# Turning x as it lands, the norm's root taken at the copy out of the in-projection, and the first conditioning chunks moved behind it

## The reference

```python
def rmsnorm(x, g):
    return x * rsqrt(mean(x * x, axis=-1) + RMS_EPS) * g

h = rmsnorm(x, g_attn_norm)                  # 256 x 1024
proj = h @ w_in                              # 1024 x 928
u, q_lat, kv_lat, k_r = split(proj, (512, 256, 128, 32))
q  = rmsnorm(q_lat,  g_q_a)  @ w_q_b         # the next product
kv = rmsnorm(kv_lat, g_kv_a) @ w_kv_b
```

## Time and profile before

| | us |
|---|---|
| median of 3 runs (lowest, highest) | 1545.74 (1544.13, 1547.88) |
| the profiled execution, device time | 1543.98 |
| its span, first to last instruction | 1542.1 |
| TensorE busy | 1459.0 (95% of the span) |
| VectorE, ScalarE, GpSimd busy | 324.6, 221.6, 21.5 |
| mean granted clock of TensorE | 0.976 |

### The profile page before, as it was taken

How to read it: one execution, slowest core, us unless ns; L and a number is a source line. 1 busy time by engine, 2 the same in 40 slices (tenths; PEclk the granted TensorE clock), 3 DMA queues, 4 the chain that set the end, 5 groups by cost and what they waited for, 6 DMA issues and landing times.

```text
span 1542.1 us, 18050 instructions
## 1 busy us (share of the span) xinstructions
PE 1459.0 (95%) x7280; PEld 791.3 (51%) x7280; DVE 324.6 (21%) x862; ACT 221.6 (14%) x405; POOL 21.5 (1%) x14
## 2 busy tenths in 40 slices
PE   7998999999999999999999999999699998999998
PEld 5654443343443343343343343343599664888843
DVE  5526321121111111121121121111323534000001
ACT  1321011011111111111011011011223420100000
POOL 3100000000000000000000000000000000000000
PEclk9998999999999999999999999999899868999999
DMA  9996999999999999999999999999844002444300
GB/s 330 357 416 272 380 427 430 428 428 429 428 428 429 428 428 429 428 428 428 428 429 429 428 428 428 428 428 408 259 156 145 28 27 83 158 143 143 131 0 27
DMA packets 82570, 496.96 MB, mean 322 GB/s; under 512 B 6237, under 2 KB 47914, under 8 KB 54666
## 3 DMA queue, kind: packets, MB, share of 16 engines
q1 hardware_dynamic: 81932, 495.46, 79.0%
q10 hardware_dynamic: 606, 1.06, 0.2%
HBM read 495.44 MB, written 1.05 MB: 322 GB/s over the span
## 4 chain that ended last, share of the span: by engine, by line
PE 61%; DMA 34%; DVE 3%; issue 1%; ACT 1%; SPq 0%; DVEq 0%; ACTq 0%
DMA ring<-in_w_gate_up_dram 33%; PE PS L816 16%; PE PS L1004 10%; PE PS L554 8%; PE PS L842 5%; PE PS L1020 5%; PE PS L802 3%; PE PS L708 3%; PE PS L850 2%; PE PS L657 2%; PE PS L537 1%; PE PS L683 1%; PE PS L510 1%; DMA ring<-in_w_ada_dram 1%; ACT work L1170 0%
## 5 line engine op out<-in xcount | busy, mean ns | idle before, releaser
L816 PE MATMUL PS<-ring,work 128*64 128x512 f32 x2048 | 450.7, 595 | 13.9 <-DMA ring<-in_w_gate_up_dram 13.9
L816 PEld LDWEIGHTS PS<-ring,work 128*64 128x64 f32 x2048 | 142.7, 137 | 304.2 <-issue 260.9
L842 PE MATMUL PS<-ring,work 128*64 128x512 f32 x1024 | 225.1, 592 | 0.0
L1643 DVE TENSOR_SCALAR work<-PS 128x512 f32<-128x512 f32 x32 | 22.1, 691 | 659.9 <-PE PS L816 659.9
L1004 PE MATMUL PS<-ring,cols 128*128 128x256 f32 x704 | 156.7, 384 | 2.1 <-issue 2.1
L1004 PEld LDWEIGHTS PS<-ring,cols 128*128 128x128 f32 x704 | 135.1, 193 | 21.0 <-DVE cols L1349 2.5
L842 PEld LDWEIGHTS PS<-ring,work 128*64 128x64 f32 x1024 | 71.6, 137 | 132.1 <-issue 129.6
L802 PE MATMUL PS<-work,rows 128*128 128x64 f32 x1056 | 124.9, 278 | 1.0 <-DVE work L1621 1.0
L802 PEld LDWEIGHTS PS<-work,rows 128*128 128x128 f32 x1056 | 123.8, 196 | 1.9 <-DVE work L1621 1.9
L554 PE MATMUL PS<-ring,cols 128*128 128x240 f32 (+3 forms) x576 | 117.1, 364 | 4.1 <-DVE cols L1349 2.1
L554 PEld LDWEIGHTS PS<-ring,cols 128*128 128x128 f32 x576 | 107.0, 190 | 12.1 <-DVE cols L1349 2.5
(11 more groups left out here) (264 smaller groups left out, 860.1 us busy)
## 6 DMA issues: line engine op xcount, KB each, us to landing
ring<-in_w_gate_up_dram SPq DMA_DIRECT2D x128, 2048.0 KB, 22.4
ring<-in_w_down_dram SPq DMA_DIRECT2D x64, 2048.0 KB, 19.5
ring<-in_w_ada_dram SPq DMA_DIRECT2D x24, 1024.0 KB, 16.9
ring<-in_w_gate_up_dram SPq DMA_DIRECT2D x22, 1024.0 KB, 5.1
ring<-in_w_in_dram SPq DMA_DIRECT2D x13, 960.0 KB, 10.8
ring<-in_w_down_dram SPq DMA_DIRECT2D x11, 1024.0 KB, 4.8
ring<-in_w_out_dram SPq DMA_DIRECT2D x8, 1024.0 KB, 10.0
ring<-in_w_in_dram SPq DMA_DIRECT2D x3, 1024.0 KB, 12.8
```

Source lines behind the costliest of these rows:

```text
L816: mm = pe.matmul(bank(b)[CAP * h:CAP * (h + 1), :], xg[:, k, :], w[:, b * FE + h * 512:b * FE + (h + 1) * 512], start=False, stop=(k == KD ...
L842: mm = pe.matmul(bank(3)[CAP * h:CAP * (h + 1), :], lhs, w[:, (f % 2) * D + h * 512:(f % 2) * D + (h + 1) * 512], start=False, stop=(f == 7))
L1643: v.tensor_scalar(g_min, bank(0), LIMIT, None, ALU.min).then_inc(clipped, 1)
```

## The change

1. x is turned on TensorE as it was loaded, half by half, without the norm (`turn_x`), and `cols` is x's transpose with the gain alone.
2. The sum of squares of the first half is taken by VectorE, that of the second by ScalarE. One inverse root of two columns is computed behind `keep_cols` and announced as `attn_r`. ScalarE applies it when it copies the in-projection's chunks out, in two instructions for a chunk (one for each half of the tokens) where it was one.
3. `cst`'s first part is loaded ahead of x.
4. `ADA_FIRST` is 0: the four w_in chunks take ring places 0 to 3, and conditioning chunks 0 to 3 take 4 to 7. TensorE computes all four between the latents' transposes and the product with w_q_b. The places from 8 on stay as they were.
5. Counts of semaphores are adapted, and `bias14_in` is merged into `gfin_in`.

```diff
-ADA_FIRST, ADA_NEXT, ADA_MID = 2, 4, 18
+ADA_FIRST, ADA_NEXT, ADA_MID = 0, 4, 18
...
+            load_small(cst[:, 0:CONST_FIRST], consts[:, 0:CONST_FIRST], "const_in")
             load_small(x_sb[:, 0, :], x_rows[:, 0, :], "x0_in")
             load_small(x_sb[:, 1, :], x_rows[:, 1, :], "x1_in")
-            load_small(cst[:, 0:CONST_FIRST], consts[:, 0:CONST_FIRST], "const_in")
...
+            def turn_x():
+
+                for t in range(NT):
+                    pe.wait_ge(sig[("x0_in", "x1_in")[t]], 16)
+                    for k in range(KD):
+                        mm = pe.transpose(bank(k // 2)[:, (k % 2) * T + t * P:][:, 0:P],
+                                          x_sb[:, t, k * P:(k + 1) * P], ident)
+                        if t == NT - 1 and k % 2:
+                            mm.then_inc(sig["rows_turned"], 1)
+                turned[0] += 1
...
             pe.wait_ge(sig["const_in"], 16)
+            turn_x()
             pe.wait_ge(sig["vec_in"], 2 * 16)
...
-            for i in range(ADA_FIRST):
-                ada(i)
...
-            turn_rows(2)
             need_cols()
             project(IN1_CHUNKS, N_IN1, (4, 5), 0)
...
+            act.wait_ge(sig["x1_in"], 16)
+            do.tell(nc.scalar.activation(rows[:, 1, :], x_sb[:, 1, :], ACT.Square,
+                                         accum_out=stat(ms, S_ATTN)[:, 1:2]), "x_squared")
             act.wait_ge(sig["vec_cols"], 1)
+            keep_cols(lambda k: col("g_attn_norm", k))
             a = VEC_ROWS["c_2"][0]
             do.tell(nc.scalar.activation(c_rep[:, :, :], vcol[:, a:a + KD].unsqueeze(2).to_broadcast([P, KD, 32]),
                                          ACT.Silu), "c_ready")
-            keep_cols(lambda k: col("g_attn_norm", k))
...
-            keep_proj(proj1, IN1_CHUNKS, (4, 5), N_IN1)
+            act.wait_ge(sig["attn_r"], 1)
+            for c, (a, w) in enumerate(IN1_CHUNKS):
+                act.wait_ge(chunk_used, N_IN1 + c + 1)
+                for t in range(NT):
+                    ins_ = nc.scalar.activation(proj1[:, t, a:a + w], bank(4 + c % 2)[:, t * w:(t + 1) * w], ACT.Copy,
+                                                scale=stat(rs, S_ATTN)[:, t:t + 1])
...
             dve.wait_ge(sig["x0_in"], 16)
-            norm_rows(S_ATTN, 0)
+            do.step(v.tensor_tensor_reduce(out=rows[:, 0, :], in0=x_sb[:, 0, :], in1=x_sb[:, 0, :], scale=1.0,
+                                           scalar=0.0, op0=ALU.mult, op1=ALU.add,
+                                           accum_out=stat(ms, S_ATTN)[:, 0:1]))
             dve.wait_ge(sig["vec_turned"], 1)
             do.tell(v.tensor_copy(vcol[:, 0:NVEC_FIRST], bank(6)[:, 0:NVEC_FIRST]), "vec_cols")
-            dve.wait_ge(sig["x1_in"], 16)
-            norm_rows(S_ATTN, 1)
             keep_cols(lambda k: col("g_attn_norm", k))
+            dve.wait_ge(sig["x_squared"], 1)
+            at = slice(0, NT)
+            src, dst = stat(ms, S_ATTN)[:, at], stat(rs, S_ATTN)[:, at]
+            do.step(v.tensor_scalar(src, src, 1.0 / D, EPS, ALU.mult, ALU.add))
+            rsqrt(dst, src, rsqrt_tmp[:, at])
+            do.tell(v.tensor_copy(dst, dst), "attn_r")
```

More of the change, by code:

```diff
@@ L152 @@
 S_ATTN, S_LAT, S_MIX, S_FFN, S_FINAL, S_NORM1, S_HEADS, S_ML, S_NORM2 = range(9)
-SIGNALS = """x0_in x1_in const_in const2_in band_in vec_in vec_a_in vec2_in pos_in wpool_in bias14_in gfin_in bada_in bgu_in bdown_in router_in
+SIGNALS = """x0_in x1_in const_in const2_in band_in vec_in vec_a_in vec2_in pos_in wpool_in gfin_in bada_in bgu_in bdown_in router_in
 brouter_in vec_turned vec_cols vec2_turned vec2_cols c_ready rows_ready rows_turned cols_dve cols_act proj_kept
@@ L160 @@
 lists_ready bias_split
-picked sel_ready selb_ready seld_ready gathered xg_ready clipped sig_ready act_ready act_turned actt_ready yb_ready
+attn_r picked sel_ready selb_ready seld_ready gathered xg_ready clipped sig_ready act_ready act_turned actt_ready yb_ready
 sel_turned selt_ready scattered
@@ L470, in _ @@
                     load_small(gfin[:, :], ins["g_final"].partition_broadcast(P), "gfin_in")
-                    load_small(bias14[:, 0:6], ins["fox_f_bias_2"][0].partition_broadcast(P), "bias14_in")
-                    load_small(bias14[:, 6:10], ins["ml_f_bias_2"][0].partition_broadcast(P), "bias14_in")
-                    load_small(bias14[:, 10:14], ins["ml_i_bias_2"][0].partition_broadcast(P), "bias14_in")
+                    load_small(bias14[:, 0:6], ins["fox_f_bias_2"][0].partition_broadcast(P), "gfin_in")
+                    load_small(bias14[:, 6:10], ins["ml_f_bias_2"][0].partition_broadcast(P), "gfin_in")
+                    load_small(bias14[:, 10:14], ins["ml_i_bias_2"][0].partition_broadcast(P), "gfin_in")
             with sp.Fori(0, EXPERTS) as e:
@@ L761, in _ @@
             pe.wait_ge(sig["x_added"], 4)
-            turn_rows(4)
+            turn_rows(2)
             ada(ADA_MID + 4)
@@ L909, in _ @@
                 add_zero(4 + 2 * t, 5 + 2 * t, start=False, stop=True).then_inc(sig["moe_done"], 1)
-            turn_rows(6)
+            turn_rows(4)
             need_cols()
@@ L981, in _ @@
             pe.wait_ge(sig["o_free"], 4)
-            turn_rows(7, by_tile=False)
+            turn_rows(5, by_tile=False)
             spread(1, 0, 0, (1,))
@@ L988, in _ @@
             pe.wait_ge(sig["gate_used"], 4)
-            turn_rows(9)
+            turn_rows(7)
             need_cols()
@@ L1083, in _ @@
             do.tell(nc.scalar.activation(trig[:, :, :, :], trig[:, :, :, :], ACT.Sin), "trig_ready")
-            keep_proj(proj1, IN1_CHUNKS, (4, 5), N_IN1)
+            act.wait_ge(sig["attn_r"], 1)
[4 more added lines that the diff above has]
+                                                scale=stat(rs, S_ATTN)[:, t:t + 1])
+                    if t:
+                        do.tell(ins_, "proj_kept")
+                    else:
+                        do.step(ins_)
             flat_q = q_rows.rearrange("p t h n -> p t (h n)")
@@ L1710, in _ @@
                         do.step(ins_)
-            dve.wait_ge(sig["gfin_in"], 16)
+            dve.wait_ge(sig["gfin_in"], 64)
             for t in range(NT):
                 do.tell(v.tensor_tensor(z_rows[t], x_sb[:, t, :], gfin[:, :], ALU.mult), "z_ready")
-            dve.wait_ge(sig["x_squared"], 2)
+            dve.wait_ge(sig["x_squared"], 3)
             r_ = rstd(S_FINAL, D)
-            dve.wait_ge(sig["x_squared"], 4)
+            dve.wait_ge(sig["x_squared"], 5)
             st = stat(ms, S_NORM1)
@@ L1744, in _ @@
             dve.wait_ge(sig["proj_kept"], len(IN1_CHUNKS) + R_GATES)
-            dve.wait_ge(sig["bias14_in"], 48)
+            dve.wait_ge(sig["gfin_in"], 64)
             def bias_of(a, n):
```

## The result

The change makes the kernel slower by a little. The medians are 1550.39 us after (1547.20 to 1557.23, 22 runs) and 1548.02 us before (1542.01 to 1552.81, 22 runs); the ratio of after to before is 1.0023, with a 95% interval of [1.0012, 1.0033], that is + 3.6 us (1.9 to 5.1). It is estimated from all 44 runs (the quotient of the two means is 1.0023 too); the quotient of the medians alone is 1.0015, or 2.4 us. The forecast was 1550.4, + 4.7. The profiled execution of after took 1548.09 us, with a span of 1546.3 against 1542.1.

A forecast was written before the change was run, and what follows sets the result against it. DMA was taken as full through the expert loop, so opening shifts carry to the end. Norm 0 + conditioning 1.9 + clock 1.9 + rotation 0.9 = + 4.7 on 1545.74 gave 1550.4 us, range 1543.5 to 1553.0.

The forecast's parts named there:

- The rest follows one to one: From w_q_b through the expert loop: a shift of the opening carries one to one to the end.
- Start of the in-projection: TensorE's opening: the first in-projection product comes at 10.1 instead of 17.11 us.
- Cold clock in the in-projection: TensorE starts the in-projection at half rate, losing 1.9 us (bounds 1.5 and 3.5); it ends at 37.3.
- The norm: Latents' norm on VectorE: squares and small steps wait for GpSimd's five instructions; done at 41.9 (was 41.95), term 0.
- Conditioning and clock behind the norm: Ahead of w_q_b: 16 more conditioning records, + 1.9, and a clock fallen in TensorE's idle stretch, + 1.9; start 48.7.
- The rotation meets GpSimd: q's rotation on VectorE: its fifth and sixth steps meet GpSimd's second part, + 0.9 us.
- clock stays up: Rival: TensorE's clock does not fall in the idle stretch; + 1.9 us, 1547.7; chance 0.25.
- only squares wait: Rival: in the latents' norm small steps pass GpSimd and only squares wait; - 0.2 us, 1545.5; chance 0.17.
- nothing small waits: Rival: neither the norm's small steps nor its products wait for GpSimd; - 2.5 us, 1543.2; chance 0.12.
- the late start: Rival: w_in transfers are fed late, so the in-projection's start isn't brought forward; + 2.6 us, 1548.3; chance 0.04.

The follow-up runs named there:

- experiment 1: Changed kernel with GpSimd's splitting of the biases held until the normalised row blocks are ready: 1543.18 us against 1548.89 before, ratio 0.9969.
- experiment 4: Changed kernel with the four conditioning chunks computed ahead of the latents' transposes, in TensorE's wait: 1546.09 us against 1548.89 before, ratio 0.9985.
- experiment 10: The changed kernel profiled once more, nothing altered: 1547.31 us.
- experiment 2: Changed kernel with GpSimd's splitting started when the norm's four squares are done, so it meets only the small steps: 1553.86 us, one run.
- experiment 3: Changed kernel with eight unused 128 x 256 products ahead of TensorE's wait for the latents: 1552.01 us, one run.
- experiment 6: Kernel of experiment 1 with two conditioning chunks instead of four ahead of w_q_b, two computed later: 1543.83 us against 1547.56 before, ratio 0.9971.
- experiment 5: Kernel before, with GpSimd's splitting held until the in-projection's row blocks are ready: 1547.79 us against 1547.56, ratio 1.0002.
- experiment 8: The kernel before profiled a second time, nothing altered: 1549.34 us.
- experiment 9: Kernel of experiment 6 with 10 unused products ahead of x's transposes and 10 ahead of the in-projection: 1540.76 us against 1548.85 before, ratio 0.9953.

## Why the prediction was right, and where it was not

**The rest follows one to one: holds, as far as one run shows.** After is 3.8 us behind at w_q_b, 3.8 at the scores, 3.77 at record 450, and 4.2 at the end of the span. In between it is between 3.3 and 6.2: from record 450 to the end the first profile of before took 1455.1 us, the third 1453.6, the second 1458.0, with the same instructions (after: 1455.5 and 1454.6). So a single profile carries some 2 us either way from stages the change doesn't touch.

**Start of the in-projection: 10.1 forecast, 11.76 measured.** The failed term is the transposes. I took 1.96 us from the earlier trace rows, where the clock was up, though the same part of the text says that TensorE starts cold: they took 3.65. That is 1.7 us, the size of the whole error; x 0.3 us later and 0.4 us less between `cols` and the first product cancel. It had no price, since the norm decides.

**Cold clock in the in-projection: 1.9 forecast, 1.7 measured** (26.99 against 25.30). The size was right and the course was not. I had TensorE begin the in-projection cold and warm up in it; in after the clock had risen at 9.04, was up at the start, and fell 0.7 us into it. Experiments 1, 4 and 10, whose TensorE list is the same up to there, go this way too (first rise at 8.97, 7.81 and 8.24). The course that I forecast came in experiments 2, 3 and 6 (first rise at 18.21, 17.36 and 17.68), and there the in-projection took 28.21, 27.92 and 28.11 us, 2.6 to 2.9 more. And the base was wrong: I charged the cold clock to after alone, but before pays it too in a part of its runs (experiments 5 and 8).

**The norm: 41.9 forecast, 42.56 measured; the mechanism is right, one count in it is not.** GpSimd started at 24.72 (24.6 forecast). VectorE's first square started 1.5 us later than forecast, for the late in-projection, and was held by the first cast already (0.89 instead of 0.42), so that four squares and one small step were spent on the five passes, where I had three squares and two steps. The number of passes decides when they end (38.96, 39.0 forecast), and how many steps they swallow decides what comes behind: 11 small steps were left where I had 7, which is about the 0.66. Experiment 2 shows that small steps wait, experiment 1 what the norm takes without GpSimd (25.98 to 31.4). The step held in after has one input, where I had counted on those with two.

**Conditioning and clock behind the norm: 48.7 forecast, 48.70 measured, with errors that cancel.** Norm to w_q_b took 6.1 us, where I had 6.8: I had added to 44.92, which held 0.46 us between the norm's end and the in-projection's, and that waiting is gone; and the clock was 1.6, not 1.9. The norm's 0.66 more made up for it.

**The rotation meets GpSimd, + 0.9: did not come.** b_down landed at 60.31 instead of 57.76, and the rotation was done at 58.67. I had left that landing where it was, but it was issued 0.9 us later (41.94 instead of 41.01) and took 1.6 us longer. In experiment 10 the meeting came, with the cast alone: the steps took 0.84 us longer and nothing was later for it. So no run shows this term as a cost. In the same way w_q_b's landing, "unchanged" at 42.35, came at 44.71. It cost nothing in after; in experiment 1 (44.9) it was the bound. A reading of mine was off besides, without effect: the earlier trace rows has the DMA engines full to the twenty-eighth slice.

**The sum.** + 4.7 was forecast, + 3.6 (1.9 to 5.1) measured. Without the rotation's 0.9 it would have been + 3.8, which is what the two first profiles differ by at w_q_b. The usual difference of the openings is smaller, about 2.9, for the mean of before's three profiles lies 0.9 us behind the first. The absolute time, 1550.4 against 1550.39, agrees by more luck than that: its base of 1545.74, from three runs, was 2.3 us below the median of 22. Of the rivals, "clock stays up" (+ 1.9) is refuted by both profiles of after, "only squares wait" and "nothing small waits" by experiment 2, the late start by the row at 11.76.

## What to carry to other kernels

When the start of a long stretch is brought forward, first find what ends beside it and only just fits: here a norm that another engine slowed down, hidden by 0.46 us. Moving work out of the front of such a chain to a place behind it is paid in full unless that second engine is moved as well; with GpSimd's splitting put later, two of the four moved chunks put behind w_q_b and TensorE kept busy at the start, the same change is worth 0.5%. And take two or three profiles of the kernel before: a base that a clock record decides moves by 2.5 us between executions of the same code.

## What the runs showed of the hardware

- A VectorE instruction of 128 x 4 elements waits for a running GpSimd instruction in full: 3.91 us instead of 0.16 with two inputs in SBUF, and also 1.74 (int32, L1334) and 1.78 us (f32, L1344) with one. The Trainium skill (SBUF — State Buffer, Who interferes with whom) says that an instruction with at most one SBUF input contends only in a two-port mode, and names `tensor_scalar` among those that can enter one; the two rows fit if so small a step is in it, which no run here tests.
- VectorE and GpSimd took turns. In experiment 2 one VectorE step passed at its usual 0.16 to 0.17 us behind each held one, and the next was held again: nine of its steps took 14.0 us, where 12 take 2.4 alone.
- The clock's first rise moved between 6.81 and 18.3 us over the kernels. With the same opening it moved by 2 us in the kernel before (12.96 to 14.91 in four executions) and by 10 us in the changed one (7.81 to 9.04 in four, 17.36 to 18.21 in three, in two of which TensorE also waited 0.24 and 0.56 us between x's halves). Whether it fell again behind that decided 1.7 us of the in-projection. TensorE busy nearly without a break from 2.85 on (experiment 9, one profile) gave the only opening with no low clock after 6.81.
- Experiment 4 shows the clock at 0.50 from 45.4, behind two idle stretches of 0.91 and 1.74 us with 0.88 us of transposes between them. So the clock also fell behind holes shorter than the 3.86 us of after.
